# Packing the small S5 matmuls of a hybrid decoder layer into row and column groups of the TensorE array

## The chip, the cores and the metric

One NeuronCore of a Trainium2 chip runs the kernel. The metric is the device time of one execution in microseconds (us), the median of several.

## The reference, cut to what matters

One layer on an input of 256 tokens by 4096 features. A combined projection of width 12296 feeds four branches: forgetting attention, stick-breaking attention, a diagonal state-space model (S5) and a gated linear recurrence (RG-LRU). Their gated outputs are joined and projected back, normalised, and added to the input. The change touches the S5 branch alone:

```
lam_bar = exp(lam * dt)                       # 64 groups x 64 states, complex
bu      = einsum('gph,blgh->blgp', b_bar, u)  # 16 inputs of a group -> 64 states
states  = scan: s[t] = lam_bar * s[t-1] + bu[t]
y       = einsum('ghp,blgp->blgh', c, states).real + d_skip * u
```

The branch has 1024 features in 64 groups of 16. A feature tile of 128 holds 8 groups, two for each value of `j` in 0..3: two groups are 2 x 16 = 32 input features and 2 x 64 = 128 states.

## The kernel before, in words

The big products go through 32 weight blocks (24 of the input projection, 8 of the output projection). Each block is streamed from memory in 16 chunks (`CH`) of 512 KB. ScalarE (ACT) rounds a chunk to its high part `w_hi` (`high`, L461), VectorE (DVE) subtracts to get the low part `w_lo` (`low`, L732), and TensorE (PE) multiplies (`chunk_fm`, L248 and L250): 8 pairs of a 128x512 and a 128x256 matmul a chunk, into the four PSUM banks of `main`. The ring has four slots, and ACT and DVE work three chunks ahead (`LEAD`): at position c of its loop each prepares chunk c + 3, once PE is through with chunk c - 1. The order on every engine is written out by hand, with semaphores between engines.

Blocks 4 to 11 (the loop at L316 on PE, L541 on ACT, L930 on DVE, L1184 and after on GpSimd, POOL) carry the S5 branch beside their own product: pass i of this loop works on feature tile i, eight passes in all. Within a pass, for each j in 0..3:

- POOL makes the rotation angles (L1189 to L1196), ACT their sines (L555 to L560), POOL the cosine (L1203);
- PE makes the two input products, real and imaginary part (L324), into bank `j % 2` of the PSUM tensor `side`: before chunks 2, 4, 7 and 10. The weights `s5_bt[:, j, r, :]` are 128x128, and only the 32 rows of this j hold anything but zeros. For j = 2 and 3 PE first waits until DVE has finished j - 2 (`s5_done`), whose bank it reuses;
- DVE rotates the inputs (L950, L951, L954, at position 2 + 3j), scans (L961, at 3 + 3j) and rotates back (L967, L968, L973, at 4 + 3j) into `s5_h[j % 2]`, and counts up `s5_done`;
- PE makes the two output products, accumulated (L339), into partitions 32j to 32j+31 of bank 2 of `side`: before chunks 7, 10, 13 and 15, each after a wait for `s5_done` of its own j.

All of these products are of plain f32. At position 15 DVE waits for ACT's copy of each bank of `main` (L472, after chunk 15), adds the bank (L872), prepares a chunk, waits for the output products (`s5_cmm`), and adds the skip term (L976). At position 0 of the next pass it copies the parameters and inputs of the next tile (L937, L938), which releases POOL and the first input products.

Bank 3 of `side` holds the forget logits from the matmuls at L310 before the loop until DVE has added their two halves (L925, `fl_dve`).

Of the kernel before, what the change touches and what calls it, by code (L numbers as in the profile page):

```python
# [10 lines left out]
ALU = mybir.AluOpType  # L11
# [4 lines left out]
T = 256  # L16
# [7 lines left out]
CH = NK // KC  # L24
# [4 lines left out]
SJ = 4  # L29
# [28 lines left out]
def hybrid_trunk(nc, x, par, bt, ct, wfg, wglu, wri, gpost, wall, out):  # L58
    ctx = ExitStack()
    with ctx:  # L60
        def sb(name, shape, dt=F32):
            return ctx.enter_context(nc.sbuf_tensor(name, shape, dt))
# [11 lines left out]
        cross = sb("cross", [P, JB, T])  # L74
# [13 lines left out]
        side = ctx.enter_context(nc.psum_tensor("side", [P, 4, BLK], F32))  # L88
# [9 lines left out]

        vflat = vals[:, :, :].rearrange("p a n -> p (a n)")
        s5_m1, s5_m2, s5_g = vflat[:, 0:512], vflat[:, 512:1024], vflat[:, 1024:1536]  # L100
        s5_h = [vflat[:, 1536:2048], vflat[:, 2048:2560]]
        s5_sin = [vflat[:, 2560:3072], vflat[:, 3072:3584]]
        s5_cos = [vflat[:, 3584:3840], vflat[:, 3840:4096]]
        rs_banks = rs_row.unsqueeze(1).to_broadcast([P, JB, T])
# [5 lines left out]
        s5_bt = scr[:, 0:1024].rearrange("p (j r s) -> p j r s", j=SJ, r=2)  # L110
        s5_ct = scr[:, 1024:1280].rearrange("p (j r h) -> p j r h", j=SJ, r=2)
        s5_cp = scr[:, 1280:1536].rearrange("p (j r h) -> p j r h", j=SJ, r=2)
        s5_u = scr[:, 1536:1792]
# [28 lines left out]
        def col(name, n=None):  # L142
# [24 lines left out]
        fl_mm, fl_act, fl_dve = sem("fl_mm"), sem("fl_act"), sem("fl_dve")  # L167
        bt_in, ct_in, p5_ready, su_ready = sem("bt_in"), sem("ct_in"), sem("p5_ready"), sem("su_ready")
        s5_tab, s5_frac, s5_trig, s5_cosd = sem("s5_tab"), sem("s5_frac"), sem("s5_trig"), sem("s5_cosd")
        s5_cq, s5_cprime = sem("s5_cq"), sem("s5_cprime")  # L170
        s5_bmm, s5_cmm, s5_dve, s5_done, s5_y = (sem(n) for n in
                                                 ("s5_bmm", "s5_cmm", "s5_dve", "s5_done", "s5_y"))
# [65 lines left out]
        def _(pe):  # L238
# [51 lines left out]
            for c in range(CH):  # L290
# [3 lines left out]
                if c == CH - 2:  # L294
# [4 lines left out]
                              stop=True).then_inc(rs_mm, 1)  # L299
# [9 lines left out]
            for k in range(NK):  # L309
                pe.matmul(side[:, 3, :], wf[:, k * FT:k * FT + P], acts[:, k, :], start=(k == 0), stop=False)  # L310
                mm = pe.matmul(side[:, 3, T:2 * T], wf[:, NK * FT + k * FT:NK * FT + k * FT + P],
                               acts[:, k, 0:T], start=False, stop=(k == NK - 1))
# [1 line left out]


            with pe.Fori(0, B_V - B_QK) as i:  # L316
                def s5_inputs(j):
                    if j == 0:
                        pe.wait_ge(su_ready, i + 1)
                        pe.wait_ge(bt_in, i * 16 + 16)  # L320
                    if j >= 2:
                        pe.wait_ge(s5_done, i * SJ + j - 1)
                    for r in range(2):
                        mm = pe.matmul(side[:, j % 2, r * T:(r + 1) * T], s5_bt[:, j, r, :], s5_u[:, :],  # L324
                                       start=True, stop=True)
                    mm.then_inc(s5_bmm, 1)

                for c in range(CH):
                    if c == 2:
                        s5_inputs(0)  # L330
                    if c in (4, 7, 10):
                        s5_inputs(c // 3)
                    if c in (7, 10, 13, 15):
                        j = (7, 10, 13, 15).index(c)
                        if j == 0:
                            pe.wait_ge(s5_cprime, i + 1)
                        pe.wait_ge(s5_done, i * SJ + j + 1)
                        for r in range(2):
                            mm = pe.matmul(side[32 * j:32 * j + 32, 2, 0:T], s5_cp[:, j, r, :],  # L339
                                           s5_h[j % 2][:, r * T:(r + 1) * T], start=(r == 0), stop=(r == 1))  # L340
                        mm.then_inc(s5_cmm, 1)
                    chunk_fm(i + B_QK, i + B_QK, c)


# [1 line left out]
            for a in range(TT):  # L346
                mm = pe.transpose(side[:, 3, a * FT:(a + 1) * FT], fl_rows[0:FT, a * P:(a + 1) * P],
                                  ident[0:FT, 0:FT])
# [4 lines left out]
            with pe.Fori(0, (B_G1 - B_V) // 2) as ii:  # L353
                for u in range(2):
                    i = ii * 2 + u
# [6 lines left out]
                    for c in range(CH):  # L362
                        for a, at in enumerate(LRU_AT):
                            if c == at + 3:
                                pe.wait_ge(wr_in, ii * 64 + (32 * u + 16 * (a + 1)))
                                pe.wait_ge(lru_v, ii * 36 + (18 * u + 9 * a + 6))
                                for r in range(2):
                                    mm = pe.matmul(side[:, 0, r * T:(r + 1) * T], lru_w[:, r, :], lru_xc[:, :],
                                                   start=True, stop=True)
# [3 lines left out]
                                for k in range(FT):  # L373
                                    mm = pe.matmul(side[:, 1, 0:T], glu_w[:, k, :], br[:, SSM0 + k, :],  # L374
                                                   start=(k == 0), stop=(k == FT - 1))
# [17 lines left out]
            with pe.Fori(0, B_G2 - B_G1) as i:  # L393
                for c in range(CH):
                    for a in range(2):
                        h = i * 2 + a
                        if c == FOX_AT[a]:
# [9 lines left out]
                                      start=False, stop=False)  # L407
                            pe.matmul(q1, at_dec[:, 2, :], later[:, :], start=False, stop=False)
                            pe.matmul(side[:, 0, 2 * P:3 * P], ident_b[:, :], causal_b[:, :],
                                      start=False, stop=True).then_inc(at_scores, 1)  # L410
# [8 lines left out]
            with pe.Fori(0, B_OUT - B_G2) as i:  # L419
                for c in range(CH):  # L420
                    for a in range(2):
                        h = i * 2 + (FT + a)
                        if c == SB_AT[a]:
# [7 lines left out]
                                      start=False, stop=True).then_inc(at_scores, 1)  # L431
# [294 lines left out]
        def _(dve):  # L726
# [203 lines left out]
            with dve.Fori(0, B_V - B_QK) as i:  # L930
                for c in range(CH):
                    if c == CH - 1:
                        sum_banks(i + B_QK)
                    low(i + B_QK, c + LEAD)
                    if c == 0:
                        dve.wait_ge(lo_ready, (i + B_QK) * CH + (LEAD + 1))
                        dve.tensor_scalar(s5_now, s5par[:, i, :], 1.0, None, ALU.mult).then_inc(p5_ready, 1)  # L937
                        dve.tensor_scalar(s5_u, br[:, SSM0 + i, :], 1.0, None, ALU.mult).then_inc(su_ready, 1)  # L938
                    if c >= 2 and (c - 2) // 3 < SJ:
                        j, part = (c - 2) // 3, (c - 2) % 3  # L940
                        g, done = i * SJ + j, i * (7 * SJ) + 7 * j
                        sin, cos, hs = s5_sin[j % 2], s5_cos[j % 2], s5_h[j % 2]
                        bu = side[:, j % 2, :]
                        if part == 0:

                            dve.wait_ge(s5_bmm, g + 1)
                            dve.wait_ge(s5_cosd, g + 1)
                            if j:
                                dve.wait_ge(s5_done, g)
                            dve.tensor_tensor(wide(s5_m1), wide(bu), both(cos), ALU.mult).then_inc(s5_dve, 1)  # L950
                            dve.tensor_tensor(wide(s5_m2), wide(bu)[:, ::-1, :], wide(sin),  # L951
                                              ALU.mult).then_inc(s5_dve, 1)
                            dve.wait_ge(s5_dve, done + 2)
                            dve.tensor_tensor(s5_m1, s5_m1, s5_m2, ALU.add).then_inc(s5_dve, 1)  # L954
                        if part == 1:

                            radius = s5_now[:, SJ + j:SJ + j + 1].to_broadcast([P, T])
                            dve.wait_ge(p5_ready, i + 1)
                            dve.wait_ge(s5_dve, done + 3)
                            for r in range(2):  # L960
                                dve.tensor_tensor_scan(s5_g[:, r * T:(r + 1) * T], radius,  # L961
                                                       s5_m1[:, r * T:(r + 1) * T], 0.0,
                                                       ALU.mult, ALU.add).then_inc(s5_dve, 1)
                        if part == 2:

                            dve.wait_ge(s5_dve, done + 5)
                            dve.tensor_tensor(wide(s5_m1), wide(s5_g), both(cos), ALU.mult).then_inc(s5_dve, 1)  # L967
                            dve.tensor_tensor(wide(s5_m2), wide(s5_g)[:, ::-1, :], wide(sin),  # L968
                                              ALU.mult).then_inc(s5_dve, 1)
                            dve.wait_ge(s5_dve, done + 7)  # L970
                            if j >= 2:
                                dve.wait_ge(s5_cmm, i * SJ + j - 1)
                            dve.tensor_tensor(hs, s5_m1, s5_m2, ALU.subtract).then_inc(s5_done, 1)  # L973
                    if c == CH - 1:
                        dve.wait_ge(s5_cmm, i * SJ + SJ)
                        dve.scalar_tensor_tensor(br[:, SSM0 + i, :], s5_u,  # L976
                                                 pars[:, bass.ds(i + PC["ssm_d"][0], 1)],
                                                 side[:, 2, 0:T], ALU.mult, ALU.add).then_inc(s5_y, 1)
                        dve.wait_ge(bank_free, i * JB + (B_QK + 1) * JB)
                        dve.scalar_tensor_tensor(br[:, bass.ds(i * JB + FOX0, JB), :], cross[:, :, :], QK_SCALE,  # L980
                                                 rs_banks, ALU.mult, ALU.mult).then_inc(br_ready, 1)
# [359 lines left out]
```

## Time and profile before

| | us |
|---|---|
| median of 3 runs | 1631.53 |
| lowest, highest | 1627.17, 1631.62 |
| span of the profiled execution | 1629.7 |
| PE busy in it | 1586.2 |
| DVE busy | 1003.4 |
| ACT busy | 820.0 |
| POOL busy | 211.2 |

The span is the time from the first to the last instruction on the core. PE's matmuls are pipelined and their ends are modelled, so that "busy" is not a count of useful columns, and starts are the surer mark. Busy shares are averages over the whole kernel: the S5 passes are a quarter of it, and what bounds them is to be read there.

### The profile page before, as it was taken

What the parts mean: (1) busy time and instruction counts of PE and PEld (TensorE: products, weight loads), DVE (VectorE), ACT (ScalarE), POOL (GpSimd) and SP (SyncE); (2) the same over time, 40 slices, a digit from 0 to 9 for tenths busy, and PEclk for the clock granted to TensorE, in tenths of its full rate; (3) what the DMA queues carried; (4) which work ended last, traced back from release to release, by engine and by line L of the source; (5) the groups of instructions that cost most, each with busy time, mean ns of one, the idle gap of its engine ahead of it and who ended that gap; (6) DMA issues with size and microseconds to landing.
All of it is one profiled execution on the core that took longest, in us unless ns stands there. A gap on an engine that the chain in (4) does not pass through costs nothing.

```text
span 1629.7 us, 24897 instructions
## 1 busy us (share of the span) xinstructions
PE 1586.2 (97%) x8228; PEld 1331.8 (82%) x8228; DVE 1003.4 (62%) x1237; ACT 820.0 (50%) x1083; POOL 211.2 (13%) x282
## 2 busy tenths in 40 slices
PE   7999999999999999999999999999999999999995
PEld 6888888777877787788888888888888888888884
DVE  6645467987798779545455554556557544444444
ACT  6643334444445444666656453466667544444442
POOL 0000052254235323000001101100000000000000
PEclk9999999999999999999999999999999999999998
DMA  8565635555555555556565545555556876666674
GB/s 291 167 181 169 204 111 171 166 163 163 159 175 151 168 171 164 178 184 196 164 210 158 165 144 187 158 170 177 162 170 187 278 211 193 193 193 193 193 233 154
DMA packets 85574, 294.38 MB, mean 181 GB/s; under 512 B 9504, under 2 KB 11808, under 8 KB 85536
## 3 DMA queue, kind: packets, MB, share of 16 engines
q1 hardware_dynamic: 77184, 276.86, 55.8%
q10 hardware_dynamic: 8352, 17.03, 3.1%
q8 instruction: 22, 0.36, 0.1%
q14 instruction: 16, 0.13, 0.0%
HBM read 289.66 MB, written 4.19 MB: 180 GB/s over the span
## 4 chain that ended last, share of the span: by engine, by line
PE 57%; issue 29%; POOL 6%; DVE 5%; ACT 3%; DVEq 0%; POOLq 0%; ACTq 0%
PE main L248 14%; PE main L269 10%; PE main L270 10%; PE main L271 10%; PE main L250 7%; PE side L374 2%; ACT w_hi L461 1%; POOL scr L1189 1%; DVE vals L961 1%; POOL scr L1192 1%; DVE vals L967 1%; DVE vals L968 1%; POOL scr L1196 1%; POOL scr L1211 1%; POOL scr L1194 1%
## 5 line engine op out<-in xcount | busy, mean ns | idle before, releaser
L732 DVE TENSOR_TENSOR w_lo<-w_raw,w_hi 128x1024 fp32r<-128x1024 f32 x512 | 642.7, 1260 | 528.6 <-ACT w_hi L461 527.6
L248 PE MATMUL main<-acts,w_hi 128*128 128x512 f32 x2560 | 915.9, 401 | 1.2 <-ACT vals L608 1.2
L461 ACT ACTIVATE w_hi<-w_raw 128x1024 fp32r<-128x1024 f32 x512 | 535.2, 1057 | 600.5 <-PE main L250 340.0
L250 PE MATMUL main<-acts,w_lo 128*128 128x256 f32 x2560 | 717.0, 280 | 0.0
L248 PEld LDWEIGHTS main<-acts,w_hi 128*128 128x128 f32 x2560 | 481.7, 188 | 128.9 <-issue 11.1
L250 PEld LDWEIGHTS main<-acts,w_lo 128*128 128x128 f32 x2560 | 484.1, 189 | 0.4
L269 PE MATMUL main<-w_hi,acts 128*128 128x512 f32 x768 | 300.7, 392 | 0.1
L271 PE MATMUL main<-w_hi,acts 128*128 128x512 f32 x768 | 298.9, 389 | 0.0
L270 PE MATMUL main<-w_lo,acts 128*128 128x512 f32 x768 | 298.8, 389 | 0.0
L269 PEld LDWEIGHTS main<-w_hi,acts 128*128 128x128 f32 x768 | 144.2, 188 | 30.5 <-DVE w_lo L732 0.5
L271 PEld LDWEIGHTS main<-w_hi,acts 128*128 128x128 f32 x768 | 144.2, 188 | 30.1
L270 PEld LDWEIGHTS main<-w_lo,acts 128*128 128x128 f32 x768 | 144.2, 188 | 29.7
L1189 POOL TENSOR_TENSOR scr<-scr,small 128x256 f32<-128x256 f32 x32 | 35.6, 1112 | 385.2 <-DVE small L937 385.2
L555 ACT ACTIVATE vals<-scr 128x256 f32<-128x256 f32 x32 | 13.4, 418 | 99.2 <-POOL scr L1196 85.6
L1224 POOL COPY scr<-br 128x256 f32 x16 | 15.6, 972 | 359.3 <-DVE small L1055 324.4
L961 DVE TENSOR_TENSOR_SCAN vals<-small,vals 128x256 f32<-128x256 f32 x64 | 47.7, 785 | 0.0
L324 PE MATMUL side<-scr 128*128 128x256 f32 x128 | 34.6, 393 | 12.6 <-DVE vals L973 12.4
L472 ACT ACTIVATE cross<-main 128x256 f32<-128x256 f32 x80 | 30.5, 381 | 22.8 <-PE main L250 22.0
L872 DVE TENSOR_TENSOR cross<-main,cross 128x256 f32<-128x256 f32 x48 | 20.1, 423 | 29.8 <-ACT cross L472 29.6
L324 PEld LDWEIGHTS side<-scr 128*128 128x128 f32 x128 | 21.7, 189 | 19.7 <-DVE vals L973 17.1
L1228 POOL COPY scr<-vals 128x256 f32 x16 | 7.4, 460 | 204.9 <-PE side L388 204.9
L339 PE MATMUL side<-vals,scr 128*32 128x256 f32 x128 | 33.6, 385 | 0.0
(232 smaller groups left out, 994.3 us busy)
## 6 DMA issues: line engine op xcount, KB each, us to landing
w_raw<-in_wall SPq DMA_DIRECT2D x512, 512.0 KB, 3.6
br<-in_x SPq DMA_DIRECT2D x16, 256.0 KB, 8.0
scr<-in_bt ACTq DMA_DIRECT2D x8, 512.0 KB, 3.3
scr<-in_wglu ACTq DMA_DIRECT2D x8, 512.0 KB, 4.1
out<-br SPq DMA_DIRECT2D x8, 512.0 KB, 3.1
br<-in_gpost ACTq DMA_DIRECT2D x8, 256.0 KB, 5.3
vals<-in_x ACTq DMA_DIRECT2D x8, 256.0 KB, 5.3
scr<-in_x ACTq DMA_DIRECT2D x8, 256.0 KB, 4.6
```

The source lines that it names most:

```text
L248: pe.matmul(main[:, j, :], w_hi[:, s, at:at + P], acts[:, k, :], start=(k == 0), stop=False)
L250: mm = pe.matmul(main[:, j, T:2 * T], w_lo[:, s, at:at + P], acts[:, k, 0:T], start=False, stop=(k == NK - 1))
L269: pe.matmul(main[:, bank0 + a, :], u_h, wh, start=(k == 0), stop=False)
L270: pe.matmul(main[:, bank0 + a, :], u_h, wl, start=False, stop=False)
L271: mm = pe.matmul(main[:, bank0 + a, :], u_l, wh, start=False, stop=(k == NK - 1))
L324: mm = pe.matmul(side[:, j % 2, r * T:(r + 1) * T], s5_bt[:, j, r, :], s5_u[:, :], start=True, stop=True)
L339: mm = pe.matmul(side[32 * j:32 * j + 32, 2, 0:T], s5_cp[:, j, r, :], s5_h[j % 2][:, r * T:(r + 1) * T], start=(r == 0), stop=(r == 1))
L374: mm = pe.matmul(side[:, 1, 0:T], glu_w[:, k, :], br[:, SSM0 + k, :], start=(k == 0), stop=(k == FT - 1))
L461: act.activation(w_hi[:, c % RING, :], w_raw[:, c % RING, :], ACT.Copy).then_inc(hi_ready, 1)
L732: dve.tensor_tensor(w_lo[:, c % RING, :], w_raw[:, c % RING, :], w_hi[:, c % RING, :].bitcast(F32), ALU.subtract).then_inc(lo_ready, 1)
L961: dve.tensor_tensor_scan(s5_g[:, r * T:(r + 1) * T], radius, s5_m1[:, r * T:(r + 1) * T], 0.0, ALU.mult, ALU.add).then_inc(s5_dve, 1)
L1189: pool.tensor_tensor(s5_a, steps_t, s5_now[:, j:j + 1].to_broadcast([P, T]), ALU.mult).then_inc(s5_tab, 1)
```

## The change: what it does

PE now makes all eight input products of a tile in one go before chunk 2, each from the 32 rows of its own j (so that weights and inputs start on partition 32j), and each j into its own bank 0 to 3 of `side`. The eight output products follow in one go before chunk 15, after one wait for all four `s5_done`; they write 32-partition groups of bank 0. The waits of j = 2 and 3 for a free bank go, on PE and on DVE. A wait for `fl_dve` is added, since bank 3 is now used. Two more state buffers `s5_h` are taken in `cross`, so that all four stay until the outputs are made. The order of the eight products is r outside, j inside.

```diff
-        s5_h = [vflat[:, 1536:2048], vflat[:, 2048:2560]]
+        cross_flat = cross[:, :, :].rearrange("p j t -> p (j t)")
+        s5_h = [vflat[:, 1536:2048], vflat[:, 2048:2560], cross_flat[:, 0:512], cross_flat[:, 512:1024]]
...
-                def s5_inputs(j):
-                    if j == 0:
-                        pe.wait_ge(su_ready, i + 1)
-                        pe.wait_ge(bt_in, i * 16 + 16)
-                    if j >= 2:
-                        pe.wait_ge(s5_done, i * SJ + j - 1)
+                def s5_inputs():
+
+                    pe.wait_ge(su_ready, i + 1)
+                    pe.wait_ge(bt_in, i * 16 + 16)
+                    pe.wait_ge(fl_dve, 1)
                     for r in range(2):
-                        mm = pe.matmul(side[:, j % 2, r * T:(r + 1) * T], s5_bt[:, j, r, :], s5_u[:, :],
-                                       start=True, stop=True)
-                    mm.then_inc(s5_bmm, 1)
+                        for j in range(SJ):
+                            rows = slice(32 * j, 32 * j + 32)
+                            mm = pe.matmul(side[:, j, r * T:(r + 1) * T], s5_bt[rows, j, r, :], s5_u[rows, :],
+                                           start=True, stop=True)
+                            if r == 1:
+                                mm.then_inc(s5_bmm, 1)
+
+                def s5_outputs():
+
+                    pe.wait_ge(s5_cprime, i + 1)
+                    pe.wait_ge(s5_done, i * SJ + SJ)
+                    for r in range(2):
+                        for j in range(SJ):
+                            mm = pe.matmul(side[32 * j:32 * j + 32, 0, 0:T], s5_cp[:, j, r, :],
+                                           s5_h[j][:, r * T:(r + 1) * T], start=(r == 0), stop=(r == 1))
+                    mm.then_inc(s5_cmm, 1)
 
                 for c in range(CH):
                     if c == 2:
-                        s5_inputs(0)
-                    if c in (4, 7, 10):
-                        s5_inputs(c // 3)
-                    if c in (7, 10, 13, 15):
-                        j = (7, 10, 13, 15).index(c)
-                        if j == 0:
-                            pe.wait_ge(s5_cprime, i + 1)
-                        pe.wait_ge(s5_done, i * SJ + j + 1)
-                        for r in range(2):
-                            mm = pe.matmul(side[32 * j:32 * j + 32, 2, 0:T], s5_cp[:, j, r, :],
-                                           s5_h[j % 2][:, r * T:(r + 1) * T], start=(r == 0), stop=(r == 1))
-                        mm.then_inc(s5_cmm, 1)
+                        s5_inputs()
+                    if c == CH - 1:
+                        s5_outputs()
                     chunk_fm(i + B_QK, i + B_QK, c)
...
-                        sin, cos, hs = s5_sin[j % 2], s5_cos[j % 2], s5_h[j % 2]
-                        bu = side[:, j % 2, :]
+                        sin, cos, hs = s5_sin[j % 2], s5_cos[j % 2], s5_h[j]
+                        bu = side[:, j, :]
...
-                            if j >= 2:
-                                dve.wait_ge(s5_cmm, i * SJ + j - 1)
                             dve.tensor_tensor(hs, s5_m1, s5_m2, ALU.subtract).then_inc(s5_done, 1)
                     if c == CH - 1:
-                        dve.wait_ge(s5_cmm, i * SJ + SJ)
+                        dve.wait_ge(s5_cmm, i + 1)
...
-                                                 side[:, 2, 0:T], ALU.mult, ALU.add).then_inc(s5_y, 1)
+                                                 side[:, 0, 0:T], ALU.mult, ALU.add).then_inc(s5_y, 1)
```

## Rows read from the trace of the kernel before

**Rows 1.** The page: span, and busy us of each engine over it.
```profile
span 1629.7 us, 24897 instructions
PE 1586.2 (97%) x8228; PEld 1331.8 (82%) x8228; DVE 1003.4 (62%) x1237; ACT 820.0 (50%) x1083; POOL 211.2 (13%) x282
```
**Rows 2.** Line L937: durations, and its first and last start in eight passes.
```profile
L937 DVE TENSOR_SCALAR small<-scr x8: 175/176/179, 218.4 to 605.3; 128x20 f32 x8
```
**Rows 3.** Windows, third pass, L937 to L937: length, then busy us by engine, clock.
```profile
328.84:384.09 55.25, 53.58 (x291) 43.47 (x290) 46.55 (x56) 25.97 (x38) 21.24 (x26) 1.00 0.54 163
```
**Rows 4.** Waits in all eight passes: who waited for whom, us in total.
```profile
PE side L324 <- DVE vals L973: 12.4, 8, 1.8
PEld main L248 <- DVE w_lo L732: 3.7, 9, 0.4
```
**Rows 5.** DVE in order of time, third pass: start, us, instruction, idle before it.
```profile
322.34 0.42 DVE L872 TENSOR_TENSOR cross<-main,cross 128x256 f32<-128x256 f32 x1 [1.86 <-ACT cross L472]
...
328.99 0.29 DVE L938 TENSOR_SCALAR scr<-br 128x256 f32 x1
334.53 3.13 DVE L732 TENSOR_TENSOR w_lo<-w_raw,w_hi 128x1024 fp32r<-128x1024 f32 x2 [5.25 <-ACT w_hi L461]
...
360.67 1.22 DVE L732 TENSOR_TENSOR w_lo<-w_raw,w_hi 128x1024 fp32r<-128x1024 f32 x1
...
373.84 0.69 DVE L973 TENSOR_TENSOR vals<-vals 128x512 f32<-128x512 f32 x1
...
377.59 0.42 DVE L872 TENSOR_TENSOR cross<-main,cross 128x256 f32<-128x256 f32 x1 [1.92 <-ACT cross L472]
```
**Rows 6.** ACT in order of time, same pass.
```profile
331.98 0.42 ACT L555 ACTIVATE vals<-scr 128x256 f32<-128x256 f32 x1 [3.78 <-POOL scr L1196]
...
377.17 0.38 ACT L472 ACTIVATE cross<-main 128x256 f32<-128x256 f32 x1 [0.83 <-PE main L250]
```
**Rows 7.** PE in order of time around chunk 15, same pass.
```profile
374.97 0.28 PE L250 MATMUL main<-acts,w_lo 128*128 128x256 f32 x1
375.18 1.05 PE L339 MATMUL side<-vals,scr 128*32 128x256 f32 x4
376.17 0.50 PE L248 MATMUL main<-acts,w_hi 128*128 128x512 f32 x1
```
**Rows 8.** PE: two starts eight pairs apart, and the wait before chunk 7.
```profile
321.73 0.40 PE L248 MATMUL main<-acts,w_hi 128*128 128x512 f32 x1
...
324.56 0.40 PE L248 MATMUL main<-acts,w_hi 128*128 128x512 f32 x1
...
347.05 1.13 PE L324 MATMUL side<-scr 128*128 128x256 f32 x4 [1.67 <-DVE vals L973]
```
**Rows 9.** Lines L324 and L339, all passes: ns min/median/max, first and last start.
```profile
L324 PE MATMUL side<-scr x128: 377/379/484, 219.7 to 635.0; 128*128 128x256 f32 x128
L339 PEld LDWEIGHTS side<-vals,scr x128: 106/110/110, 237.7 to 652.1; 128*32 128x32 f32 x128
L339 PE MATMUL side<-vals,scr x128: 379/379/404, 237.7 to 652.3; 128*32 128x256 f32 x128
```
**Rows 10.** PE at the kernel's start: an idle stretch and two pairs of chunk 0.
```profile
10.47 1.11 PE L283 MATMUL side<-ident,br 128*128 128x128 f32 x4 [3.38 <-DMA br<-in_x]
...
12.02 0.63 PE L248 MATMUL main<-acts,w_hi 128*128 128x512 f32 x1
...
12.66 0.63 PE L248 MATMUL main<-acts,w_hi 128*128 128x512 f32 x1
...
15.86 0.43 PE L248 MATMUL main<-acts,w_hi 128*128 128x512 f32 x1
```
**Rows 11.** Windows of 1 us after the last matmul: busy us by engine, clock next to last three.
```profile
1613.00:1614.00 1.00, 0.30 (x2) 0.00 (x0) 0.39 (x1) 0.67 (x2) 0.00 (x0) 1.00 0.00 0
...
1616.00:1617.00 1.00, 0.00 (x0) 0.00 (x0) 0.93 (x3) 0.00 (x0) 0.00 (x0) 0.88 0.00 0
1617.00:1618.00 1.00, 0.00 (x0) 0.00 (x0) 1.00 (x2) 0.00 (x0) 0.00 (x0) 0.50 0.00 0
```

## The prediction

> **What bounds the kernel now.** The page comes first: PE is busy 97% of the span [rows 1], so the change seems to cut where it counts. But it touches only the eight S5 passes, and these have to be read by themselves. Line L937 runs once a pass; its first and last start give (605.3 - 218.4) / 7 = 55.27 us a pass [rows 2]. What PE has to do in one: 16 chunks of 324.56 - 321.73 = 2.83 us [rows 8] are 45.3 us, and eight groups of small products at some 0.9 to 1.0 us (an output group with its change of shape takes 376.17 - 375.18 = 0.99 us [rows 7]) are 7.6. That is 52.9 of 55.27, so PE idles some 2.4 us a pass, and the list of waits says for whom: 12.4 us over eight passes for DVE's L973, the end of a state, and almost nothing for weights [rows 4]. DVE is busy 46.55 us of a pass [rows 3], which looks like slack. Its order of time says otherwise: after L938 it stands 5.25 us, because ACT waits for POOL's angles, and POOL for L937 [rows 5, 6]; from 334.53 to the end of L973 at 374.53 it has no idle stretch over 0.24 us; then it waits 1.92 us for the copy of the first bank of chunk 15 and goes on to L937 of the next pass [rows 5]. So a pass is a ring: L937, POOL, ACT, 40 us of DVE, the last state, PE's last output products, chunk 15, ACT's copy L472, L872, L937. PE stands in this ring only from the last state to the first bank of chunk 15: 374.53 to 377.59 is 3.06 us of 55.27. Whatever PE saves elsewhere in the pass becomes waiting.
>
> **The change, part by part.** *Input products, j = 1 to 3 moved to chunk 2.* They left PE's time before chunks 4, 7 and 10, where it was early or waited for DVE anyway. At chunk 2 DVE doesn't need their results for some 8 us (L938 ends at 329.28; DVE first stands idle, and then prepares two chunks until 337.66 before it rotates [rows 5]). They may take 0.9 us, as one group now, if four go at once, or 3.5 if none do; chunks 3 and 4 come later by the difference, and ACT's chunk 3 + 3 waits for chunk 2, but ACT is held by POOL until 331.98 [rows 6], so at most some tenths of a us reach it, in a stretch where its work lies ahead of DVE's. I take 0, with 0 and +0.3 us a pass as ends. *Waits for a free bank, and `fl_dve`.* The first were met by the same `s5_done` that the output products waited for; they go, and what is late next is the chunk's low part from DVE. `fl_dve` is met before the first pass needs it. Behind it only PE's own chunks are queued. 0. *States in `cross`.* DVE's own writes, the same size; ACT writes `cross` after chunk 15, when PE has read them. 0. *The first three output groups moved to chunk 15.* Here lies what counts. Before, PE came to this point at about 375.18, later than the state at 374.53 [rows 5, 7]. Now it comes early: chunk 12 needs the low part that DVE ends at 360.67 + 1.22 = 361.89 [rows 5], three chunks of 2.83 end at 370.38, and PE waits 4.2 us for the last state. It resumed within 0.1 us of a state at 347.05 [rows 8]; so the outputs start at 374.59 instead of 375.18: -0.59 us a pass.
>
> What then stands before chunk 15 is eight products where there were two. Each f32 product shows as two matmul records: 128 for 8 passes x 8 products [rows 9]. Four records last 1.05 us with 0.379 for the last, so they start (1.05 - 0.379) / 3 = 0.224 us apart [rows 7, 9]. The trace has no two products of different groups side by side, so the price is bounded from both sides:
> - all four groups side by side: 4 records deep, as now, +0;
> - none side by side: 16 records deep, 12 x 0.224 = +2.69 us.
>
> Between them lies a value that follows from the order in the code. The two records of a product use the same part of the array and can't overlap; the next product is behind them in the queue. If it starts no earlier than the second record of its forerunner, each product adds one step instead of two: A1, A2 with B1, B2 with C1, and so on, 9 steps for eight products, +5 x 0.224 = +1.12 us. The weight loads of the outputs give almost the same: 16 loads of 0.11 us [rows 9] are 1.76 us if they don't overlap, against 0.9 for four records. I take +1.12. The sum is -0.59 + 1.12 = +0.53 us a pass, and 8 x 0.53 = +4.2 us; with the ends, 8 x (-0.59) = -4.7 and 8 x (-0.59 + 2.69) = +16.8 us.
>
> The profiled execution has a span of 1629.7 us, between the runs' lowest, 1627.17, and their median, 1631.53; its own time isn't listed, so the difference is put on the median: 1635.7 us.
>
> The Trainium skill bears on this in "TensorE: Matmul & The Clock Gate", Packing small matmuls: tiles on different groups start some 4 ns apart, three column groups gave 2.38 times the rate. By that the sum would be near -4.7 us. The same section says that matmuls start and end strictly in program order, which is what makes the nine steps of an f32 pair plausible; no row here shows either.
>
> **The rivals.** *Full overlap.* For it: 32 rows or columns are separate parts of the array. Against it: two records a product on one part, and separate moving data for each column group, which nothing here shows running at once. It gives 1631.5 - 4.7 = 1626.8 us, at the edge of what can be told.
>
> *No overlap: the change doesn't do what it says.* For it: plain f32 products in two records, and not one overlap of them in this trace. The place is the stretch from last state to chunk 15, the price 2.69 - 0.59 = 2.1 us a pass, and it decides as soon as the group is over 0.59 us longer than now. 1631.5 + 16.8 = 1648.3 us, although PE would have no more to do in total than before.
>
> *The clock.* PE's work is concentrated and its waiting too. After the last matmul, at 1613.3, PE idles, and the granted clock drops within 1616 to 1617 (0.88 is about three quarters of that window at full) to 0.50, that is 1.2 GHz, some 3.5 us after PE stopped [rows 11]. At the start, after 3.38 us of idling, pairs come 12.66 - 12.02 = 0.64 us apart, half rate, and are back at full by 15.86 [rows 10]. The new wait of 4.2 us is longer than both; the longest now doesn't lower the clock (1.00 over the pass [rows 3]). If it falls, outputs and chunk 15 run at half rate, just in the ring: some 4.6 us at half rate, as at the start, cost 2.3 us a pass. In all eight passes, on top of the forecast, that is +18.4: 1654 us; in two or three, +5 to +7: 1641. Against it: the wait ends about when the clock would fall, and a matmul is then there again. The Trainium skill, "TensorE: Matmul & The Clock Gate", The HAM clock gate, has the same rule, that the low clock is the default and activity lifts it; it speaks against a change that lumps PE's idle time together, and these rows agree with it.
>
> *PE bound after all.* If DVE's 40 us shrank as PE steps aside (another meeting of DVE with POOL, whose operations in this stretch vary in length), up to the 1.92 us that DVE waits could go too. I see no cause.
>
> **How the numbers follow.** Half overlap, clock kept in most passes: 0.37. Full overlap: 0.25. No overlap: 0.20. The clock falling in most passes: 0.12. Something else, either way: 0.06. A difference under 0.3% (4.9 us) can't be told from none. Of the likeliest (+1 to +8 us, 1632 to 1640) some seven tenths are within it, the rest slower; of full overlap half is within, half faster; the other two are slower. Faster 0.16, within 0.42, slower 0.42. The range goes from full overlap, 1626, to a little above no overlap, 1651; beyond it lie full overlap with another gain, and the clock falling throughout.
>
> **What would show it.** PE starts the output group within 0.1 us of the last L973, after a wait of about 4 us; the time from its first record to chunk 15 is 1.0 us (full), 2.1 (half) or 3.7 (none); the pass is 55.8 us (54.7, 57.4); DVE's stretch from the first chunk to the last L973 stays at 40 us; PE's waits for DVE grow from 1.6 to over 6 us a pass. The granted clock is 1.00 in the windows over chunk 15, or 0.5 to 0.9 if the clock rival holds. The forecast is wrong if DVE's stretch gets shorter by over half a us, or if PE's new waits spread over the chunks instead of standing before the outputs.

## The result, and the profile after

The changed kernel takes 1644.18 us (median of 4 runs, 1643.06 to 1644.70), the kernel before 1631.21 (4 runs): +13.0 us, ratio 1.0078, 95% interval 1.0065 to 1.0091. It is slower, clear of noise. The time lies in the range, but well above the forecast of 1635.7, and by other steps than the likeliest case had.

The page, to be set against [rows 1]: PE is busy 20 us less, the span is 13 us longer.

```profile
span 1642.9 us, 24857 instructions
PE 1566.6 (95%) x8228; PEld 1317.9 (80%) x8228; DVE 1003.9 (61%) x1237; ACT 818.4 (50%) x1083; POOL 210.5 (13%) x282
```

The line that copies the parameters, L941 now, against [rows 2]: (615.4 - 217.8) / 7 = 56.80 us a pass, where it was 55.27. Eight times the difference is 12.2 us, so the S5 passes hold nearly all of it.

```profile
L941 DVE TENSOR_SCALAR small<-scr x8: 175/176/179, 217.8 to 615.4; 128x20 f32 x8
```

PE around chunk 15 of the first pass (start, us, instruction, idle before it), against [rows 7]:

```profile
259.19 0.28 PE L251 MATMUL main<-acts,w_lo 128*128 128x256 f32 x1
263.54 0.41 PE L337 MATMUL side<-vals,scr 128*32 128x256 f32 x2 [4.06 <-DVE cross L975]
263.55 0.41 PE L337 MATMUL side<-cross,scr 128*32 128x256 f32 x2
263.78 0.39 PE L337 MATMUL side<-vals,scr 128*32 128x256 f32 x2
263.79 0.39 PE L337 MATMUL side<-cross,scr 128*32 128x256 f32 x2
263.99 0.39 PE L337 MATMUL side<-vals,scr 128*32 128x256 f32 x2
264.01 0.39 PE L337 MATMUL side<-cross,scr 128*32 128x256 f32 x2
264.21 0.39 PE L337 MATMUL side<-vals,scr 128*32 128x256 f32 x2
264.22 0.39 PE L337 MATMUL side<-cross,scr 128*32 128x256 f32 x2
264.54 0.79 PE L249 MATMUL main<-acts,w_hi 128*128 128x512 f32 x1
...
265.34 0.63 PE L249 MATMUL main<-acts,w_hi 128*128 128x512 f32 x1
...
265.98 0.63 PE L249 MATMUL main<-acts,w_hi 128*128 128x512 f32 x1
```

Two things are to be seen. The sixteen records of the eight products start in four steps of 0.22 us, four at a time: full overlap, and 264.54 - 263.54 = 1.00 us until chunk 15 against 0.99 before. And the pairs of chunk 15 come 0.64 us apart, which was 0.35: half clock. The windows of the same place (length, busy us by engine, clock third from the end) show it fall at 264.54, 1.0 us after PE resumed (a mean of 0.77 is 0.54 us at full clock and 0.46 at half), and come back at 267.94, 3.4 us later:

```profile
264.00:265.00 1.00, 1.00 (x13) 0.59 (x6) 0.62 (x1) 0.00 (x0) 0.00 (x0) 0.77 0.72 295
265.00:266.00 1.00, 1.00 (x5) 0.81 (x5) 0.00 (x0) 0.00 (x0) 0.00 (x0) 0.50 0.33 33
...
267.00:268.00 1.00, 1.00 (x5) 0.85 (x4) 0.14 (x2) 0.38 (x1) 0.00 (x0) 0.53 0.75 307
```

It falls in all eight passes, around waits of 3.9 to 4.1 us each, but not always alike. In the second pass it has fallen at 319.14, before PE resumes, and comes back at 325.98:

```profile
319.75 0.64 PE L337 MATMUL side<-vals,scr 128*32 128x256 f32 x2 [3.91 <-DVE cross L975]
...
321.61 0.80 PE L249 MATMUL main<-acts,w_hi 128*128 128x512 f32 x1
```

```profile
319.00:320.00 1.00, 0.25 (x4) 0.20 (x8) 0.99 (x2) 0.00 (x0) 0.00 (x0) 0.57 0.66 131
...
325.00:326.00 1.00, 1.00 (x4) 0.86 (x4) 0.42 (x1) 0.14 (x1) 0.00 (x0) 0.51 0.00 0
```

That is 6.8 us of half clock, 6.2 of them with PE at work, and the eight products take 321.61 - 319.75 = 1.86 us instead of 1.00. Passes 1, 3 and 6 are of the first kind, 3.4 us of half clock, and last 56.2 us; passes 2, 4, 5 and 7 of the second, 5.1 to 6.2 us of it with PE at work, and last 57.0 to 57.5. (The eighth is of the second kind too.)

In DVE's order of time, in the first pass again, the last state ends at 262.79 + 0.69 = 263.48 and PE resumes 0.06 us later; the four bank additions, evenly 0.71 us apart before, are late ([rows 5] has the first):

```profile
262.79 0.69 DVE L975 TENSOR_TENSOR cross<-vals 128x512 f32<-128x512 f32 x1
...
266.64 0.42 DVE L876 TENSOR_TENSOR cross<-main,cross 128x256 f32<-128x256 f32 x1 [2.02 <-ACT cross L476]
267.92 0.43 DVE L876 TENSOR_TENSOR cross<-main,cross 128x256 f32<-128x256 f32 x1 [0.85 <-ACT cross L476]
...
269.61 0.42 DVE L876 TENSOR_TENSOR cross<-main,cross 128x256 f32<-128x256 f32 x1 [0.28 <-ACT cross L476]
```

The input products cost little: sixteen records in 220.21 - 219.13 = 1.08 us in all.

```profile
219.13 1.15 PE L326 MATMUL side<-scr 32*128 32x256 f32 x16
220.21 0.51 PE L249 MATMUL main<-acts,w_hi 128*128 128x512 f32 x1
```

### The profile page after: what moved, and what is told of

Read it like the earlier page. It is cut to its first block, busy times and chain, and to the rows that moved or that the text cites. A ratio compares the mean times of both kernels' runs of the same rounds, so it can differ in the third digit from the quotient of the medians.

```text
span 1642.9 us, 24857 instructions
## 1 busy us (share of the span) xinstructions
PE 1566.6 (95%) x8228; PEld 1317.9 (80%) x8228; DVE 1003.9 (61%) x1237; ACT 818.4 (50%) x1083; POOL 210.5 (13%) x282
## 4 chain that ended last, share of the span: by engine, by line
PE 55%; issue 30%; DVE 6%; POOL 6%; ACT 3%; DVEq 0%; POOLq 0%; ACTq 0%
PE main L249 13%; PE main L272 10%; PE main L271 10%; PE main L270 10%; PE main L251 7%; PE side L378 2%; DVE vals L965 1%; POOL scr L1191 1%; ACT w_hi L465 1%; POOL scr L1194 1%; DVE vals L971 1%; DVE vals L972 1%; POOL scr L1198 1%; POOL scr L1213 1%; POOL scr L1196 1%
## 5 line engine op out<-in xcount | busy, mean ns | idle before, releaser
L249 PE MATMUL main<-acts,w_hi 128*128 128x512 f32 x2560 | 927.9, 405 | 15.4 <-DVE w_lo L736 13.1
L249 PEld LDWEIGHTS main<-acts,w_hi 128*128 128x128 f32 x2560 | 487.5, 190 | 152.9 <-DVE w_lo L736 32.4
L251 PEld LDWEIGHTS main<-acts,w_lo 128*128 128x128 f32 x2560 | 489.9, 191 | 0.0
L337 PE MATMUL side<-vals,scr 128*32 128x256 f32 x64 | 14.5, 603 | 31.8 <-DVE cross L975 31.8
L337 PEld LDWEIGHTS side<-vals,scr 128*32 128x32 f32 x64 | 4.3, 152 | 37.8 <-DVE cross L975 34.4
L1198 POOL TENSOR_TENSOR scr<-scr 128x256 f32<-128x256 f32 x32 | 32.6, 1019 | 2.5
```

Of the source, the lines that this page charges most:

```text
L249: pe.matmul(main[:, j, :], w_hi[:, s, at:at + P], acts[:, k, :], start=(k == 0), stop=False)
L251: mm = pe.matmul(main[:, j, T:2 * T], w_lo[:, s, at:at + P], acts[:, k, 0:T], start=False, stop=(k == NK - 1))
L1198: pool.tensor_tensor(s5_f, s5_a, s5_k, ALU.subtract).then_inc(s5_frac, 1)
```

## The experiments

The theory after the result: a ring through DVE, POOL, ACT and PE's chunk 15 sets the pass; the packing takes PE out of its way (-0.6 us a pass); but PE's waiting is now one stretch of 4 us, and the half clock that comes with it lies in the ring (+2.3). The rivals: the lump of eight products before chunk 15 costs by itself, or the inputs at chunk 2 do. All experiments below were timed beside the kernel before, whose median was 1630.4 to 1631.3 then.

### PE kept busy before the outputs: 14 and 6 filling matmuls

```diff
                 def s5_outputs():
+                    pe.wait_ge(s5_done, i * SJ + SJ - 1)
+                    for n in range(14):                      # or 6
+                        pe.matmul(side[:, 1, :], wf[:, 0:P], acts[:, n, :], start=True, stop=True)
                     pe.wait_ge(s5_cprime, i + 1)
                     pe.wait_ge(s5_done, i * SJ + SJ)
```

> The changed kernel, with 14 matmuls of 128x512 (f32r, into bank 1 of side, results unused) put before the output products, after a wait for the third state, so that PE is idle for about 1.2 instead of 4.1 us before them. Theory (clock): the loss is the half clock over the outputs and chunk 15, which follows the idle stretch; it stays at 1.00, the pass gets shorter than before's 55.27 by the 0.59 us at which PE used to come late: 54.7 us, 1626 to 1627 us in all. Rival (the lump itself: eight products before chunk 15, whatever the clock): it stays at 1644, or more by the filler. Rival (the power that dense work draws, more work makes it worse): clock still under 1.

Measured: 1625.68 us, ratio 0.9967 (0.9958 to 0.9976). Three more microseconds of work on PE in each pass made the kernel 18.5 us faster than the changed one. Its second pass, PE in order of time, and its parameter copy, (602.2 - 219.4) / 7 = 54.69 us a pass:

```profile
315.61 3.38 PE L335 MATMUL side<-acts,wf 128*128 128x512 f32 x14
319.83 0.41 PE L340 MATMUL side<-vals,scr 128*32 128x256 f32 x2 [0.84 <-DVE cross L978]
...
320.83 0.50 PE L249 MATMUL main<-acts,w_hi 128*128 128x512 f32 x1
```

```profile
L944 DVE TENSOR_SCALAR small<-scr x8: 175/176/177, 219.4 to 602.2; 128x20 f32 x8
```

The idle stretch before the outputs is 0.84 us, and the clock is 1.00 over chunk 15 of every pass. The rival of the lump is out: all eight products still stand before chunk 15, and the group still takes 1.00 us.

> As with 14, but 6 filling matmuls: about 1.3 us of work, some 2.7 to 2.8 us of idling left before the outputs. Theory (clock): shorter than the idle stretches that were followed by half clock (3.4 us and up), so the clock stays and the time is that of 14: 1626 to 1628. If the sum of activity matters and not one unbroken stretch, some passes still fall, 1630 to 1640. Rival (the lump itself): 1644.

Measured: 1630.24 us, ratio 0.9997 (0.9986 to 1.0008), no different from before. The wait was 2.5 to 2.7 us in each pass. In the profiled execution the clock fell in three of the eight and stayed in the others. This is the last of the three, the seventh pass:

```profile
594.00:595.00 1.00, 0.25 (x4) 0.20 (x8) 1.00 (x2) 0.00 (x0) 0.00 (x0) 0.83 0.77 131
595.00:596.00 1.00, 1.00 (x12) 0.39 (x8) 0.83 (x1) 0.00 (x0) 0.00 (x0) 0.50 0.89 360
```

The theory's stronger form, that 2.5 us are safe, fell; the weaker one, some passes, is what happened. Those three passes took 56.2 to 56.3 us, the others 54.7. The eleven runs range from 1623.2 to 1631.9, and their times follow the mean granted clock of each run: 0.996 in the fastest (1623.2, as in kernels whose clock is kept), 0.995 in two of 1627.6 and 1627.7, 0.992 or 0.993 in the eight of 1629.7 to 1631.9. So a spread of 9 us among runs of one program goes with how often its clock falls.

### One half of the change alone, and the outputs in two groups

Inputs packed, outputs where they were:

```diff
                     if c == 2:
                         s5_inputs()                          # all eight, as in the change
-                    if c == CH - 1:
-                        s5_outputs()
+                    if c in (7, 10, 13, 15):
+                        s5_output((7, 10, 13, 15).index(c))  # two products, after s5_done of this j
```

> The input products packed before chunk 2 on row groups, the output products as before: one group of two before each of chunks 7, 10, 13 and 15. Theory (ring and clock): PE now reaches chunk 15 before the last state, so -0.59 us a pass; its idling is split into pieces of under 2.5 us before several chunks, the clock stays: 1626 to 1627 us. Rival (the inputs at chunk 2 cost, by the later chunks 2 to 4): 1632 to 1644.

Measured: 1624.71 us, ratio 0.9972 (0.9961 to 0.9983), 54.65 us a pass. The time came out 1.3 us under the forecast of 1626 to 1627; the forecast of the clock failed. PE now waits 2.0 to 2.1 us before chunk 7, and in the profiled execution the clock falls there, in the second to eighth pass, for 3.4 us each (the mean over a window of 4 us is 0.58 to 0.68 in each); the third pass:

```profile
344.87 1.05 PE L337 MATMUL side<-vals,scr 128*32 128x256 f32 x4 [1.98 <-DVE vals L976]
345.85 0.79 PE L249 MATMUL main<-acts,w_hi 128*128 128x512 f32 x1
```

```profile
345.00:346.00 1.00, 1.00 (x5) 0.38 (x4) 1.00 (x1) 0.57 (x2) 0.40 (x1) 0.90 0.02 8
...
348.00:349.00 1.00, 1.00 (x4) 0.81 (x4) 1.00 (x2) 0.00 (x0) 0.92 (x2) 0.50 0.53 176
```

It costs nothing in the length of a pass, 54.65 us as with the clock kept: chunk 7 isn't in the ring, and PE has caught up by chunk 15, where it starts the output products at 372.41 in the third pass, 0.05 us after the last state's end at 372.36. A stretch of 3.4 us at half clock is worth 0 here and 1.5 us in the changed kernel's passes of 56.2, by where it lies. That is the plainest evidence for the ring. (Two of the seven runs had a mean clock of 0.996, so hardly a fall, and took 1624.7 and 1623.2 us; the four at 0.989 took 1624.7 to 1627.2. Whether the falls cost a us or two outside the passes' length isn't settled by so few.)

Outputs packed before chunk 15, inputs as in the kernel before:

```diff
-                    if c in (7, 10, 13, 15):
-                        ...
+                    if c == CH - 1:
+                        ...                                  # all eight outputs, into bank 2
```

> The output products together before chunk 15 on column groups, the input products as before (four groups of two, 128 rows, plain). Theory (ring and clock): PE is early for chunk 15 again, by some 3 to 4 us, and most or all passes fall to half clock: 1638 to 1645 us. If the stretch is a little shorter than in the changed kernel, only some passes fall. Rival (inputs cost): the loss goes away, 1627 to 1632.

Measured: 1624.23 us, ratio 0.9969 (0.9958 to 0.9980). This expectation was wrong. The waits before the outputs were 1.6 to 1.9 us, not 3 to 4, because the inputs of j = 2 and 3 still wait for a free bank before chunks 7 and 10 and take part of PE's idling there, as in the third pass; the clock stayed at 1.00 over chunk 15 in all passes.

```profile
344.22 1.13 PE L325 MATMUL side<-scr 128*128 128x256 f32 x4 [1.64 <-DVE vals L971]
354.91 1.13 PE L325 MATMUL side<-scr 128*128 128x256 f32 x4 [1.24 <-DVE vals L971]
...
371.76 0.41 PE L339 MATMUL side<-vals,scr 128*32 128x256 f32 x2 [1.85 <-DVE cross L971]
```

So each half alone gains 6 us, and both together lose 13: the bank waits that the change removed, and the input products behind them, kept the idle stretch short. Which of the two did more wasn't tested.

Both halves, the outputs in two groups:

```diff
-                    if c == CH - 1:
-                        s5_outputs()
+                    if c == CH - 3:
+                        s5_outputs((0, 1, 2))
+                    if c == CH - 1:
+                        s5_outputs((3,))
```

> The changed kernel with the output products in two groups: j = 0, 1, 2 together before chunk 13, j = 3 alone before chunk 15. The lump of PE's waiting (4.1 us before chunk 15) is cut into about 1.4 and 1.8 us. Theory (clock): no half clock over chunk 15, pass 54.7 us, 1624 to 1627. Rival (eight products need to be in one lump to gain, or the loss is from the inputs at chunk 2): 1631 to 1644.

Measured: 1625.79 us, ratio 0.9959 (0.9946 to 0.9973), 54.66 us a pass, waits of 1.5 us before chunk 15, clock 1.00 there. PE's other wait, before chunk 13, is 1.1 to 1.2 us. It mends the change with its packing kept.

### Overlap: the order of the products, and none at all

```diff
-                    for r in range(2):
-                        for j in range(SJ):
+                    for j in range(SJ):
+                        for r in range(2):
                             mm = pe.matmul(side[32 * j:32 * j + 32, 0, 0:T], ...
```

> The kernel with 14 filling matmuls, whose clock stays at full, with the output products in the other order: j outside, r inside, so that four records of one column group follow each other. Theory A (groups side by side by themselves, PE starts a later product of a free group past an earlier one that waits for its group): as fast as with r outside, pass 54.69 us, 1625.7. Theory B (records start in program order, a later one waits): 13 steps of 0.21 instead of 4, +1.9 us a pass, 56.6 us, 1641.

Measured: 1626.67 us, ratio 0.9976 (0.9967 to 0.9985), 54.71 us a pass. Four records of one column group now follow each other in the program, and still four groups start together, the first record of each before the second of any:

```profile
317.59 0.42 PE L340 MATMUL side<-vals,scr 128*32 128x256 f32 x2 [0.85 <-DVE cross L978]
317.62 0.42 PE L340 MATMUL side<-cross,scr 128*32 128x256 f32 x2
317.83 0.39 PE L340 MATMUL side<-vals,scr 128*32 128x256 f32 x2
```

Theory A holds. My own reason for half overlap, that a waiting record holds up the groups behind it, is refuted.

All eight outputs in one column group (the outputs of j = 1 to 3 are thereby left out of the result):

```diff
-                            mm = pe.matmul(side[32 * j:32 * j + 32, 0, 0:T], ...
+                            mm = pe.matmul(side[0:32, j, 0:T], ...
```

> The kernel with 14 filling matmuls, with all eight output products in the first column group (partitions 0 to 31) of four different banks, so that none can lie beside another; three quarters of the S5 outputs are then left out of the sum. It measures the rival of no overlap at full clock. Theory (ring): the group takes 16 steps of 0.21 to 0.22 us instead of 4, +2.6 us in the ring, pass 57.3 us, 1625.7 + 21 = 1646 to 1647. Rival (not in the ring, hidden by the idling of PE): 1626.

Measured: 1647.15 us, ratio 1.0105 (1.0087 to 1.0122); (615.8 - 215.0) / 7 = 57.26 us a pass. Four records of each group one after the other, 378.84 - 375.27 = 3.57 us until chunk 15:

```profile
375.27 1.05 PE L340 MATMUL side<-vals,scr 128*32 128x256 f32 x4 [0.86 <-DVE cross L978]
376.16 1.03 PE L340 MATMUL side<-cross,scr 128*32 128x256 f32 x4
377.02 1.03 PE L340 MATMUL side<-vals,scr 128*32 128x256 f32 x4
377.89 1.03 PE L340 MATMUL side<-cross,scr 128*32 128x256 f32 x4
378.84 0.50 PE L249 MATMUL main<-acts,w_hi 128*128 128x512 f32 x1
```

The group is 2.57 us longer and the pass as well: what is put between the last state and chunk 15 is paid in full. The overlap itself is worth 21 us here, at full clock.

### The ring opened: the parameter copy at position 14

The first tile's parameters are copied before the loop; `s5par_next` is `s5par` shifted by one tile, its entry behind the last tile set to 0. In these kernels a pass is measured from one copy of the inputs (the former L938) to the next.

```diff
                     if c == 0:
                         dve.wait_ge(lo_ready, (i + B_QK) * CH + (LEAD + 1))
-                        dve.tensor_scalar(s5_now, s5par[:, i, :], 1.0, None, ALU.mult).then_inc(p5_ready, 1)
...
+                    if c == CH - 2:
+                        dve.tensor_scalar(s5_now, s5par_next[:, i, :], 1.0, None, ALU.mult).then_inc(p5_ready, 1)
```

> The kernel before, with one link of the ring moved: DVE copies the next tile's parameters (the small copy that releases POOL's angles) at position 14 instead of position 0 of the next pass. Theory (the passes are bound by the ring DVE, POOL, ACT, DVE): the 3.8 us wait of ACT and the 5.25 us wait of DVE go or shrink; the next bound is PE's own 52.9 us a pass: 53 to 53.5 us instead of 55.27, 1612 to 1617 in all. Rival (PE was the bound all along, busy 97%): no change, 1631.

Measured: 1615.01 us, ratio 0.9901 (0.9883 to 0.9919), 53.27 us a pass. A 0.18 us copy moved on DVE, with PE's instructions unchanged, gains 15 to 16 us on a PE that was "97% busy". Here PE is the bound: in these passes its trace has no idle stretch over 0.05 us.

> The changed kernel with the same early copy. Theory (ring and clock): PE has only 45.3 + 2.1 = 47.4 us of work in a pass now, DVE 46.5 busy and 2 to 3 of waiting for the last banks: some 49.5 us a pass, 1631 - 8 x 5.8 = 1585 if the clock stays, 1597 if it still falls in the passes. So the packing is worth 25 us or more once the ring is open. Rival (packing gains nothing, or the clock takes all): not faster than the kernel before with the early copy.

Measured: 1624.18 us, ratio 0.9959 (0.9944 to 0.9974): faster than without the copy by 20 us, but slower than the kernel before with it. It came out as the rival said, "the clock takes all": waits of 3.7 to 4.1 us before the outputs in every pass, and half clock as PE resumes. My figure for just that case, 1597, was 27 us too low: it took 49.5 us for the pass with the clock kept, where the three kernels below show 52.1, and the falling clock brings that to 52.9 to 54.7.

```profile
427.00:428.00 1.00, 0.90 (x12) 0.45 (x16) 1.00 (x2) 0.00 (x0) 0.00 (x0) 0.50 0.85 340
```

> Inputs packed, outputs in four groups of two as before, and the early copy of the parameters. Theory (ring): with the clock kept over chunk 15 the ring is the 40 us of DVE, its 5 us of chunk preparation, 2.5 us from the last state to the first bank and what is left of the waits at position 0: some 51 to 51.5 us a pass, and PE's work is 45.3 + 1.1 + 4 x 1.0 = 50.4, just under it: 1597 to 1602 us. Rival (the packing is worth nothing even with the ring open): as the kernel before with the early copy, 1615.

> Outputs packed before chunk 15, inputs as before (four plain groups), and the early copy. Theory (ring): PE's work is 45.3 + 4 x 0.9 + 1.0 = 49.9 us, ring 51 to 51.5: 1597 to 1602, the same as with the inputs packed. If PE's idle stretch before the outputs is over some 2.5 us and the clock falls, 1610 or more.

> All products packed, outputs in two groups (three and one) before chunks 13 and 15, and the early copy. Theory (ring and clock): PE's work is 45.3 + 1.1 + 2 x 1.0 = 48.4, the ring 51 to 51.5 us: 1597 to 1602, no faster than the two half packings, since the ring binds all three. Rival (PE's work still counts): 8 x 1.5 us faster than them, 1585 to 1590. If the clock falls in the ring: 1615 and more.

Measured: 1605.79 (ratio 0.9846, 0.9832 to 0.9859), 1606.98 (0.9849, 0.9836 to 0.9863) and 1604.01 us (0.9828, 0.9814 to 0.9841). At least five of the seven passes between copies of the inputs are 52.05 to 52.10 us long in each of them (the others 51.4 to 51.7), somewhat longer than the 51 to 51.5 expected, so that the times are 2 to 5 us above my figures. PE idles 2.4 to 2.7 us a pass in the third and 0.3 to 0.9 in the first, with the same pass: the ring, not PE, binds them. The third pass of the third kernel had DVE busy 46.57 of 52.08 us (third figure); the most of what is left is two waits for ACT's high parts, of 1.64 and 1.37 us, and 1.24 us for the first bank. So with the ring open the packing is worth another 11 us (1615.0 to 1604.0), where it was worth 5 to 6 before. The third is the fastest kernel of this study, 27 us under the one before; the differences among the three lie within their intervals.

```profile
321.49:373.57 52.08, 49.39 (x290) 40.53 (x289) 46.57 (x56) 26.12 (x39) 21.29 (x27) 1.00 0.59 175
```

## Why the prediction was right or wrong, point by point

*The ring bounds the pass, and PE's saving elsewhere turns into waiting:* right. With the clock kept and the overlap, every version without the early copy takes 54.65 to 54.71 us a pass, whatever PE has to do; the sum without any cost had 55.27 - 0.59 = 54.68. DVE's stretch from its first chunk to the last state is 40.0 us in every pass of both kernels, as forecast. PE's own work was put a little low: 52.9 us, where the kernel with the early copy, bound by PE, takes 53.27; and PE idled 1.7 us in a pass (55.25 - 53.58 in [rows 3]) rather than 2.4. PE's waits for DVE grew to 5.6 us a pass, not to over 6, and 1.6 of them lie before chunks and not before the outputs (us in total over the eight passes, times, longest):

```profile
PE side L337 <- DVE cross L975: 31.8, 8, 4.1
PE main L249 <- DVE w_lo L736: 13.1, 16, 1.2
```

*-0.59 us, as PE comes early to chunk 15:* right; PE resumed 0.06 us after the state, and the wait was 3.9 to 4.1 us against 4.2 forecast.

*Inputs at chunk 2, free banks, `fl_dve`, states in `cross`, at 0:* right as far as the time of a pass shows it; the group took 1.08 us. (The wait that goes on DVE was for a free state buffer, not for a bank.) One thing was missed: the wait for a free bank cost nothing, but it was useful, since it broke up PE's idling (outputs alone).

*"If it starts no earlier than the second record of its forerunner", +1.12 us:* the step that failed first. Where the clock was full the value was +0.01 (1.00 against 0.99 us), four groups side by side in either order. The other case had its rule from the Trainium skill, "TensorE: Matmul & The Clock Gate", Packing small matmuls: near-simultaneous starts on different groups. This trace agrees with it: the two rows of each step, of two records each, start 0.01 to 0.02 us apart. The same section's word on strict program order, which I leaned on, doesn't hold for starts across groups here: with the other order of the products the first records of the third and fourth group, ninth and thirteenth in the program, stand in the row at 317.62, before the second record of any group (317.83). The measurement decides.

*The clock, put at 0.12 as a rival:* the step that failed second, by its chance. It fell in all eight passes. The price was close in the mean: 2.3 us forecast, (1644.18 - 1625.68) / 8 = 2.3 us measured against the filled kernel, 56.80 - 54.69 = 2.1 by the two traces. But it is the mean of two kinds, 1.5 us for the short stretches and 2.3 to 2.8 for the long ones, where the forecast had one of 4.6 us at half rate. My reason against it was that the wait ends about when the clock would fall, and a matmul is then there again. Both halves were wrong. In the fourth pass PE stopped at 429.59 (its wait of 3.90 us ends at 433.49), and the clock fell at 431.78, 2.2 us later; in the first it fell 5.1 us after PE had stopped, when matmuls had been running for 1.0 us.

```profile
431.00:432.00 1.00, 0.00 (x0) 0.00 (x0) 1.00 (x2) 0.00 (x0) 0.00 (x0) 0.89 0.85 319
```

And the stretch at the kernel's start in [rows 10] was no second case of a fall. The matmuls of L283 start 0.21 us apart both before those 3.38 us and after them, and 0.11 us apart only at 16.25 us: PE had been at half rate all along.

```profile
5.15 1.94 PE L283 MATMUL side<-ident,br 128*128 128x128 f32 x8 [5.15 <-DMA br<-in_x]
...
16.25 0.60 PE L283 MATMUL side<-ident,br 128*128 128x128 f32 x4
```

Full overlap and the falling clock together give 1631.2 - 4.7 + 18.4 = 1644.9, within a microsecond of the result. Both prices stood in the prediction, but no case joined them; the rivals were set on top of the half overlap alone. That the time fell into the range, and on the slower side, is luck: two errors of opposite sign, -9.0 us for the overlap (8 x 1.12), +18.4 for the clock.

## What to carry to other kernels

Before work is taken off the busiest engine, follow the ring that sets the loop's period; here PE was in it for 3 of 55 us, and a small copy moved on another engine was worth 16 us where the packing by itself was worth 5 to 6. Work that is packed packs its waiting too: look where the idle time gathers, and keep a long wait on TensorE away from the stretch that others wait for, by splitting the group or by leaving a cheap wait elsewhere. Give each pair of rivals that can hold together a line of its own in the sum.

## What the runs showed of the hardware

Plain f32 matmuls on four 32-column groups ran side by side with all 128 rows moving in each: sixteen records in 1.00 us, 3.57 us in one group. On 32-row groups with 128 columns, sixteen took 1.08 us, where four of 128 rows took 1.07 ([rows 8], from 347.05 to the outputs at 348.12). On the column groups, neither of two orders in the program made a difference.

The granted clock fell to half around idle stretches of TensorE of 3.7 to 4.1 us every time (sixteen of sixteen passes), of 2.5 to 2.7 us in three of eight, and of 2.0 to 2.1 us before chunk 7 in seven of seven. It didn't around those of up to 1.9 us. The length of the stretch alone doesn't decide. All fourteen kernels share an idle stretch of 2.10 to 2.16 us some 60 us from the start, long before the first S5 pass: half clock came with it in the traces of four (14 filling matmuls; outputs in two groups; the early copy in the changed kernel, and with the outputs packed alone) and not in those of the other ten. Here are the kernel before and, second, the one with 14 filling matmuls:

```profile
60.74 0.67 PE L298 MATMUL side<-scr,later 128*128 128x256 f32 x2 [2.15 <-DVE scr L859]
60.20 1.19 PE L299 MATMUL side<-scr,later 128*128 128x256 f32 x2 [2.16 <-DVE scr L866]
```

```profile
61.00:62.00 1.00, 1.00 (x7) 0.86 (x7) 1.00 (x2) 0.00 (x0) 0.00 (x0) 1.00 0.76 307
61.00:62.00 1.00, 1.00 (x4) 0.81 (x4) 0.61 (x2) 0.00 (x0) 0.00 (x0) 0.50 0.82 336
```

What else decides was not tested. In the changed kernel a fall came 2.2 to 5.1 us after TensorE had stopped, before or after it was at work again, and the half clock lasted 3.4 us (in three passes) or 6.8 us (in five). Over the first 15.9 us of the kernel the views show a granted clock of 1.00 while the matmuls come at half rate; there the starts are to be trusted.
